# Stick-breaking attention: the factors 1-beta stay in PSUM for the scan, and GpSimd makes the low halves of q and k

## The reference, cut to what matters

```
logits = einsum('bthd,bshd->bhts', q_blk, k) * scale
log_beta      = log_sigmoid(logits)
log_one_minus = where(causal, log_beta - logits, 0.0)
suffix  = cumsum(log_one_minus, axis=3, reverse=True) - log_one_minus
weights = where(causal, exp(log_beta + suffix), 0.0)
out     = einsum('bhts,bshd->bthd', weights, v)
```

## Time and profile before

| | us |
|---|---|
| median of 3 runs | 2876.29 (2876.2 to 2882.55) |
| the profiled execution | 2885.02 |
| its span, first to last instruction | 2883.3 |
| attention in it | 1753 to 2494, 741 us |
| PE busy over the span | 2628.2 (91%) |
| DVE busy over the span | 1745.1 (61%) |

### The profile page before, as it was taken

One profiled execution on the slowest core, in us unless ns is written; L12 is line 12 of the kernel. 1 busy time (PEld: TensorE's weight loads), 2 busy tenths in 40 slices (PEclk: granted clock), 3 DMA queues, 4 the chain that ended last, 5 costly groups with the idle time before them and its releaser, 6 DMA issues. The chain is left out here.

```text
span 2883.3 us, 39017 instructions
## 1 busy us (share of the span) xinstructions
PE 2628.2 (91%) x13800; PEld 2234.5 (77%) x13800; DVE 1745.1 (61%) x2113; ACT 1269.1 (44%) x2234; POOL 911.1 (32%) x726
## 2 busy tenths in 40 slices
PE   4999999999799999999969996877888888799998
PEld 3888888888688888888859995666766666689897
DVE  6545555455655555555534446999999999643343
ACT  5654333343455333343322113766767676421111
POOL 3443333223544333233312115444444444100000
PEclk8999999999999999999979997999989899899999
DMA  3333333333222333333354441112111121343332
GB/s 95 88 117 109 99 110 116 113 110 102 80 88 81 101 113 115 115 103 108 113 176 126 140 153 51 63 41 73 65 44 68 40 68 63 117 161 117 109 109 73
DMA packets 239710, 283.54 MB, mean 98 GB/s; under 512 B 12048, under 2 KB 189200, under 8 KB 236560
## 3 DMA queue, kind: packets, MB, share of 16 engines
q1 hardware_dynamic: 229008, 265.86, 28.9%
q10 hardware_dynamic: 10624, 16.78, 1.6%
HBM read 190.32 MB, written 92.27 MB: 98 GB/s over the span
## 5 line engine op out<-in xcount | busy, mean ns | idle before, releaser
L584 PE MATMUL in_bank<-in_a_hi,in_w_hi 128*128 128x512 f32 x2016 | 791.4, 393 | 29.9 <-ACT in_o L390 17.6
L586 PE MATMUL in_bank<-in_a_lo,in_w_hi 128*128 128x512 f32 x2016 | 788.3, 391 | 0.0
L587 PE MATMUL in_bank<-in_a_hi,in_w_lo 128*128 128x512 f32 x2016 | 788.1, 391 | 0.0
L584 PEld LDWEIGHTS in_bank<-in_a_hi,in_w_hi 128*128 128x128 f32 x2016 | 381.2, 189 | 111.9 <-ACT in_o L390 18.5
L1391 DVE TENSOR_TENSOR_SCAN att_rest<-att_rest 128x512 f32<-128x512 f32 (+3 forms) x320 | 446.0, 1400 | 33.4 <-ACT att_rest L1343 30.9
L1302 POOL TENSOR_TENSOR att_slot<-att_slot,att_rest 128x512 f32<-128x512 f32 (+3 forms) x320 | 343.0, 1077 | 373.7 <-DVE att_rest L1391 373.7
L587 PEld LDWEIGHTS in_bank<-in_a_hi,in_w_lo 128*128 128x128 f32 x2016 | 380.9, 189 | 79.8
L586 PEld LDWEIGHTS in_bank<-in_a_lo,in_w_hi 128*128 128x128 f32 x2016 | 381.2, 189 | 78.6
L480 DVE TENSOR_TENSOR in_w_lo<-carried_buffer,in_w_hi 128x512 fp32r<-128x512 f32 x216 | 247.9, 1148 | 264.1 <-ACT in_w_hi L381 261.2
L381 ACT ACTIVATE in_w_hi<-in_sums 128x512 fp32r<-128x512 f32 x288 | 181.4, 631 | 486.1 <-PE in_bank L587 333.8
L281 POOL TENSOR_TENSOR in_sums<-carried_buffer 128x512 f32<-128x512 f32 x72 | 95.0, 1319 | 692.7 <-DMA carried_buffer<-in_w_in 692.7
(11 more groups left out here) (139 smaller groups left out, 4755.5 us busy)
## 6 DMA issues: line engine op xcount, KB each, us to landing
carried_buffer<-in_w_in SPq DMA_DIRECT2D x144, 512.0 KB, 4.8
uz_T<-in_o SPq DMA_DIRECT2D x32, 256.0 KB, 4.0
va_T<-in_o SPq DMA_DIRECT2D x32, 256.0 KB, 3.8
q_T<-in_o SPq DMA_DIRECT2D x32, 256.0 KB, 3.6
k_T<-in_o SPq DMA_DIRECT2D x32, 256.0 KB, 3.6
vb_T<-in_o SPq DMA_DIRECT2D x32, 256.0 KB, 3.5
zb_T<-in_o SPq DMA_DIRECT2D x32, 256.0 KB, 3.6
ga_T<-in_o SPq DMA_DIRECT2D x32, 256.0 KB, 3.5
```

What stands on the lines that cost most here:

```text
L584: pe.matmul(bank[:, :], hi, a_hi[:, i, k], start=opens and k == 0, stop=False, skip_group_check=True)
L586: pe.matmul(bank[:, :], hi, a_lo[:, i, k], start=False, stop=False, skip_group_check=True)
L587: mm = pe.matmul(bank[:, :], lo, a_hi[:, i, k], start=False, stop=k == HALF_K - 1, skip_group_check=True)
```

## The change

Four edits, all in `attention`:

1. ACT writes `sigmoid(-z)` back over the logits in the same PSUM bank instead of into `rest`. Its semaphore is now called `rest_done`. The wait for `weighted` (that `rest[i % 4]` is free) goes from ACT to DVE.
2. The scan takes data0 from that PSUM bank and writes into `rest` in SBUF; data1, which the operation `bypass` doesn't use, is one column of ones in SBUF, broadcast to the width.
3. PE may overwrite a bank of `z_ps` when it has been scanned, no longer when ACT has read it.
4. The low halves of q and k for the next head (8 quarters for each of seven heads, 56 of the 64) are made on POOL, behind the weights in its order; those of the first head stay on DVE.

```
-                act.activation(rest[i % RESTS][:, right:right + width], src, ACT.Sigmoid, scale=-SCALE)\
-                    .then_inc(z_read, 1)
+                act.activation(src, src, ACT.Sigmoid, scale=-SCALE).then_inc(rest_done, 1)
...
+            def rest_qk(h, part):
+                pool.wait_ge(qk_hi, len(SPLITS) * h + part + 1)
+                (src, hi, lo), cols = quarter(part)
+                pool.tensor_tensor(lo[:, cols], src[:, cols], hi[:, cols].bitcast(F32), ALU.subtract)\
+                    .then_inc(qk_done, 1)
...
             def scan(i, at, width, h, n):
-                dve.wait_ge(z_read, PIECES * h + (n + 1))
                 left = S - (i + 1) * P + at
                 r = rest[i % RESTS]
                 if at + width < (i + 1) * P:
                     dve.wait_ge(scanned, PIECES * h + n)
-                backwards = r[:, left:left + width][:, ::-1]
-                dve.tensor_tensor_scan(out=backwards, data0=backwards, data1=backwards,
+                elif i >= RESTS:
+                    dve.wait_ge(weighted, PIECES * h + pieces_before(i - RESTS + 1))
+                elif not first_head(h):
+                    dve.wait_ge(weighted, PIECES * h + (pieces_before(NT + i - RESTS + 1) - PIECES))
+                dve.wait_ge(rest_done, PIECES * h + (n + 1))
+                backwards = z_ps[n % Z_BANKS][:, 0:width][:, ::-1]
+                dve.tensor_tensor_scan(out=r[:, left:left + width][:, ::-1], data0=backwards,
+                                       data1=r[:, S:S + 1].to_broadcast([P, width]),
                                        initial=r[:, left + width:left + width + 1], op0=ALU.mult,
                                        op1=ALU.bypass).then_inc(scanned, 1)
...
                 if before >= 0 or not first_head(h):
-                    pe.wait_ge(z_read, PIECES * h + (before + 1))
+                    pe.wait_ge(scanned, PIECES * h + (before + 1))
```

More of the change, by code:

```diff
@@ L1171, in attention @@
         z_full = sc.sem("z_full")
-        z_read = sc.sem("z_read")
+        rest_done = sc.sem("rest_done")
         scanned = sc.sem("scanned")
@@ L1309, in body @@
                         weights(*e[1:], h + 1, FIRST + n - PIECES)
+                    elif e[0] == "QK":
+                        rest_qk(h + 1, e[1])
             for n, e in enumerate(early):
@@ L1330, in sigmoids @@
                 w = (i + 1) * P
-                right = S - w + at
                 act.wait_ge(z_full, PIECES * h + (n + 1))
@@ L1376, in _, with first_rest_qk @@
         def _(dve):
-            def split_qk(h, part):
-                dve.wait_ge(qk_hi, len(SPLITS) * h + part + 1)
+            def first_rest_qk(part):
+                dve.wait_ge(qk_hi, part + 1)
                 (src, hi, lo), cols = quarter(part)
@@ L1411, in body @@
                         scan(*e[1:], h + 1, FIRST + n - PIECES)
-                    elif e[0] == "QK":
-                        split_qk(h + 1, e[1])
                     elif e[0] in "VB":
@@ L1430, in _ @@
             for part in range(len(SPLITS)):
-                split_qk(0, part)
+                first_rest_qk(part)
             for n, e in enumerate(early):
```

## The result

The changed kernel takes 2757.41 us (median of 4 runs, 2756.26 to 2759.53) against 2878.9 us for the kernel before in the same runs: a ratio of 0.9581, 95% interval 0.9568 to 0.9594, 121 us less. The forecast was 2789 us, that is 87 us less, with a range of 2757 to 2828. The direction and what the scan and the low halves do were right; the gain is about four tenths larger than forecast, and the time lies only 0.4 us inside the range's lower end.

A forecast was written before the change was run, and what follows sets the result against it. DVE was taken to bound attention; afterwards PE and DVE nearly tie, with 80.5 instead of 91.4 us a head. Six heads 65, head 0 8, early pieces 11, last head 3: 87 off 2876.3 gives 2789 us, range 2757 to 2828.

The forecast's parts named there:

- The ring: PE's three logits banks, held through the scan: no limit between products, 1.17 to 1.37 us a piece in early pieces.
- The pause at k0: PE's wait for k0's low half at the turn to the next head's logits: 3.2 us at least, 4 taken.
- The clock behind it: PE at its lower clock level after the k0 pause: 2.7 us lost a head now, 2.5 taken after the change.
- The larger of the two in each stretch makes 71.3 us: Head's base time: the larger of PE's and DVE's work in each of four stretches, totals 68.4 and 66.8 us.
- the four V: Stretch 1 of a head: the chain of the four V, about 2 us of idle DVE, stays: 2 us.
- don't mesh fully: Charge in each head for equally loaded engines in a common order: 0.4 us a stretch, 1.5 us.
- my last correction: Head's sum cut from 81.3 to 80.5 us, as PE was priced 15.9 us against 14.95 in one stretch.
- Head 0: The first head, 88.7 us before the change, was to gain 8 us.
- C: Rival, chance 0.10: no pause beyond 3.2 us, clock at its upper level, 75 us a head, 2751 us.
- A: Rival, chance 0.12: scan still suffers under POOL by its output or SBUF start column; only part 3 gains, 2827 us.
- B: Rival, chance 0.08: the ring of three banks bites within heads, 0.15 us a piece, 6 us a head, 2836 us.
- D: Rival, chance 0.04: scan dear from PSUM, at 2.15 us a wide scan 101 us a head, slower, 2953 us.

The follow-up runs named there:

- k0 ahead of POOL's last weights: Changed kernel with POOL making k0's low half before, not after, its weights for the head's last piece: 2733.42 us.
- The cheap scan: Changed kernel with the scan replaced by a plain product of the same operands, the running product left out: 2730.56 us.
- both edits at the turn: Changed kernel with k0's low half ahead of POOL's last weights and QK_REST = 12 instead of 3: 2729.32 us, ratio 0.9483 to the kernel before.
- data1 in PSUM: Kernel before with only the scan's unused data1 read from the logits' PSUM bank, held until scanned: 2781.28 us, ratio 0.9665.
- part 4 alone: Kernel before with only the wait changed, so PE may overwrite a logits bank only once it is scanned: 2874.16 us, ratio 0.9979.
- one constant of the order: Changed kernel with QK_REST = 12 instead of 3, putting three turns with products between k0 and its logits: 2735.05 us.

## Why the prediction came out as it did

**Right, with the size.** Scan from PSUM: 1.28 us taken, 1277 ns measured, on 224 of them. The Trainium skill ("VectorE: DVE Perf Modes", the errata section) gives VectorE 120 fixed cycles with a PSUM source and 58 with an SBUF one, by estimate 65 ns more for a scan. No row shows that: 1277 ns with data0 in PSUM and 1271 ns with data1 there, against the 1.28 us of an undisturbed scan that reads only SBUF. ACT into PSUM: no cost. Low halves on POOL: 1.2 us taken, 1.28 and 1.29 measured. `weighted` on DVE: not in the list of waits. The ring: 0 in heads, early pieces 29.4 us where I had 28 to 29. The pause at k0: 4 us taken, 3.95 measured, for POOL as I had it. The clock behind it: 2.5 us taken. On PE's timeline, the first logits after the pause:

```profile
2119.20 0.47 PE L1449 MATMUL att_z_ps<-att_k_hi,att_q_hi 128*128 128x128 f32 x1 [3.95 <-POOL att_k_lo L1307]
...
2121.41 0.63 PE L1494 MATMUL att_y_ps<-att_wT_lo,att_v_hi 128*128 128x512 f32 x1
...
2124.50 0.34 PE L1495 MATMUL att_y_ps<-att_wT_hi,att_v_lo 128*128 128x384 f32 x1
```

From 2119.2 to about 2124.2 PE works at the lower level (0.63 us for 512 columns instead of 0.39), 5.0 us with half the work lost: 2.5.

One reading was too simple: the scans of the kernel before do not come in just two durations. Its wide scans spread from 1.27 to 2.15 us, with 1.46, 1.65 and 2.01 among them. The sum used the mean of 1598 ns and was not hurt by it.

**The step that failed** is "The larger of the two in each stretch makes 71.3 us", with two charges behind it, "2" for the four V and "1.5" because engines "don't mesh fully". In a head of 75.04 us there are the pause 3.95, the clock 2.5 and 1.0 of waiting for V. What is left for PE's own work is 67.6 us. The kernel with k0 ahead of POOL's last weights says the same in a head at full clock: 70.9 - 2.2 - 1.0 = 67.7. PE's price by my rows was 68.4, so that term was good to 1%. But I took 71.3 for it: 3.7 too much. The charge for the V was 1.0 too much and the one for meshing 1.5, less the 0.8 of my last correction: 5.4 us a head in all, the difference between 80.5 and 75.0. The `Y` that bound the stretches are marks on DVE, no barriers: PE worked ahead across them. In stretch 1 I had PE 10.0 and DVE 12.9 us; in the trace PE is busy there for 12.76 of 13.8 us, and in stretch 4 for 24.5 where I had 26.5: the same work, cut at another place. With a head's total, PE 68.4 + 3.95 + 2.5 + 1.0 = 75.9, the forecast would have been 4.6 us a head nearer. My last correction, 81.3 to 80.5, even saw that PE was priced high in one stretch, and cured it by 0.8.

The cheap scan is the test of it: if stretches where DVE is longer had cost 2.9 us a head, taking 17 us from DVE would have given these back beside the shorter pause and wait for V (1.4 + 0.6 us) and the clock; it gave 2.7 in all, and its head less its pause, wait and clock is PE's 67 to 68 us again.

This account has a limit. In the kernel with both edits at the turn PE runs at the full clock, and its waits in a head (for DVE's subtractions, in five places) sum to about 1.9 us. So 67.6 us of own work would make 69.5, and the head is 71.0. Where those 1.5 us go is not known; the charge for engines that don't mesh, nothing in the changed kernel, may not be nothing there.

**Luck in the total.** The gain was summed from the traced execution of 2885.0 us but taken off the median, 2876.3. Trace against trace the change saved 127.8 us where the sum had 87, a miss of 41 us. Beside the forecast of 2789 it looks like 32, because the base was 8.7 us lower. With the same range about a forecast of 2798, the time would have lain outside it.

**Head 0** was put at 8 us and gave 15.0: the same miss, 87.8 to 72.8 us, no new cause. The last head: 3 forecast, 3.7 measured.

**The rivals.** C (fewer losses than charged, 75 us a head, 2751) is closest in the number, by luck: neither pause nor clock was smaller, its reason did not occur. A (the scan still suffers) is refuted by the row of scans. The Trainium skill ("SBUF — State Buffer", Who interferes with whom) goes by the number of inputs that a VectorE instruction has in SBUF, and the column of ones in SBUF (1603 ns) and data1 in PSUM (1271 ns) agree with it, from both sides. B and D did not occur: no wait for a scan within heads, and no scan above 1284 ns.

**Which part paid.** My sum gave 9.0 + 1.5 us a head to the scan and 8.0 to the move, as if independent. They are not: 95 and 25 us with the scan first, and at most 0.3% of the time for the move without it.

**Open.** Why the granted clock stays up in every second head of the kernel with a 2.19 us pause and falls in the others, where the work is the same, I did not try to find out. Heads of two lengths occur with part 4 alone too, 91.3 and about 89.2 us; whether it is the same thing is open as well.

## What to carry to other kernels

The scan, with two tensor operands in SBUF, was stretched by POOL's work here. So look for durations of the same shape that spread (1.27 to 2.15 us here) before moving work to POOL, and first take one operand to PSUM, even an unused one. When two engines come out equal, sum each over a whole period and don't add up maxima over stretches that no barrier closes. After a large gain look at the one pause left in the period: here 4 us of it cost 6.5 with the clock behind it, one constant of the order gave half of that back (3.3 us a head), and both edits 4.1. And take a gain off the same execution that it was read from.

## What was not expected of the hardware

- An operand that the operation bypasses counts in full: a broadcast column of ones in SBUF leaves the scans at 1603 ns, a PSUM operand in its place makes them 1271 ns.
- The collision costs both sides, and POOL more when POOL has more to do: its wide weights take 1093 ns without it, 1158 in the kernel before, 1371 with the low halves on POOL as well.
- A subtraction of two SBUF tensors of 512 columns takes 1.28 to 1.29 us on POOL, the product that overwrites its own input 1.09 us, both undisturbed. What makes the difference was not tested.
- With the same pause of 2.19 us in each head the granted clock was 1.00 in every second head and 0.98 in the others.
